# Early expert loads, padded rows left out of the gathers, shorter routing and a reordered end in a two-block transformer kernel

## What is computed

```
x = x + hybrid_mixer(rmsnorm(x))              # ends with the product y @ w_out
h = rmsnorm(x, norm_ffn_g)
grp = argmax(h @ rg_w + rg_b)                 # 1 of 4 groups
top_val, top_idx = top_k(expert logits of that group, 2)      # 2 of its 8 experts
gate = p_grp * softmax(top_val)
x = x + sum over the 2 picks: gate * (silu(h @ w_gate[e]) * (h @ w_up[e])) @ w_down[e]
out = rmsnorm(x, final_norm_g)
```

## Time and profile before

| | us |
|---|---|
| median of 3 runs | 2107.6 |
| lowest and highest of them | 2099.24, 2107.98 |
| the profiled execution, as a run | 2113.0 |
| its span in the trace | 2111.7 |

### The profile page before, as it was taken

The page is one execution under the profiler, slowest core; times in us unless marked ns, Lnnn a source line. Parts: engine busy times, 40 slices in busy tenths (PEclk is TensorE's granted clock), DMA queues, the critical chain, the costliest instruction groups (busy, mean ns, idle before and its releaser), DMA issues.

```text
span 2111.7 us, 24139 instructions
## 1 busy us (share of the span) xinstructions
PE 1889.9 (89%) x8578; PEld 1303.9 (62%) x8578; DVE 836.9 (40%) x1154; ACT 409.2 (19%) x740; POOL 969.0 (46%) x492
## 2 busy tenths in 40 slices
PE   5999999899998999999999799967589799988882
PEld 4888888787776778888888467645533333333330
DVE  5444433310444576444534797783500000100003
ACT  3111100100344422111100435523111011111011
POOL 5888887677544478888877143211110000100001
PEclk9999999999999999999999899988689899999996
DMA  3333382322111133333322122101799999999983
GB/s 125 98 99 93 103 339 99 131 90 90 60 51 50 52 94 94 96 92 99 105 96 89 44 88 60 60 30 30 301 351 391 391 396 373 388 388 399 387 359 129
DMA packets 59729, 359.60 MB, mean 170 GB/s; under 512 B 7136, under 2 KB 7520, under 8 KB 47648
## 3 DMA queue, kind: packets, MB, share of 16 engines
q1 hardware_dynamic: 45216, 317.21, 42.0%
q10 hardware_dynamic: 10192, 27.32, 3.4%
q0 software_dynamic: 4272, 14.42, 2.2%
HBM read 384.36 MB, written 27.00 MB: 195 GB/s over the span
## 4 chain that ended last, share of the span: by engine, by line
PE 70%; DMA 13%; DVE 11%; ACT 3%; issue 1%; POOL 1%; SPq 0%; DVEq 0%; ACTq 0%; POOLq 0%
PE bank L448 30%; DMA big<-w_up_in 12%; PE bank L419 11%; PE bank L1683 9%; PE bank L680 4%; PE bank L1236 3%; PE bank L1698 3%; DVE big L1013 3%; PE bank L467 2%; PE bank L1344 2%; PE bank L598 1%; DVE state L998 1%; PE bank L658 1%; ACT work L614 1%; PE bank L1624 1%
## 5 line engine op out<-in xcount | busy, mean ns | idle before, releaser
L265 POOL TENSOR_TENSOR weights_hi_parts<-ring,ones 128x1024 fp32r<-128x1024 f32 (+1 forms) x176 | 356.3, 2024 | 308.7 <-PE bank L448 138.8
L267 POOL TENSOR_TENSOR ring_parts<-ring,weights_hi_parts 128x1024 fp32r<-128x1024 f32 (+1 forms) x176 | 473.7, 2692 | 13.8
L448 PE MATMUL bank<-attention_buffers_parts,weights_hi_parts 128*128 128x512 f32 x832 | 329.5, 396 | 28.4 <-POOL ring_parts L267 17.8
L448 PE MATMUL bank<-state_parts,weights_hi_parts 128*128 128x512 f32 x832 | 326.8, 393 | 0.0
L448 PE MATMUL bank<-attention_buffers_parts,ring_parts 128*128 128x512 f32 x832 | 326.7, 393 | 0.0
L1683 PE MATMUL bank<-big,work 128*64 128x512 f32 x1040 | 295.9, 624 | 27.0 <-DMA big<-w_up_in 26.8
L419 PE MATMUL bank<-big_parts,weights_hi_parts 128*128 128x512 f32 x704 | 217.1, 390 | 1.2 <-POOL ring_parts L267 1.2
L1768 POOL TENSOR_TENSOR small<-small 128x1 f32<-128x1 f32 x36 | 6.9, 193 | 434.8 <-DVE small L1629 434.8
L448 PEld LDWEIGHTS bank<-attention_buffers_parts,weights_hi_parts 128*128 128x128 f32 x832 | 158.0, 190 | 65.1 <-POOL ring_parts L267 17.8
L852 POOL TENSOR_TENSOR ring_parts<-ring,weights_hi_parts 128x1024 fp32r<-128x1024 f32 x32 | 80.8, 2527 | 234.5 <-ACT weights_hi_parts L849 234.5
L1683 PEld LDWEIGHTS bank<-big,work 128*64 128x64 f32 x1040 | 103.3, 144 | 129.5 <-issue 121.3
(11 more groups left out here) (347 smaller groups left out, 2683.9 us busy)
## 6 DMA issues: line engine op xcount, KB each, us to landing
ring<-wdense_in SPq DMA_DIRECT2D x176, 512.0 KB, 3.6
big<-w_up_in SPq DMA_DIRECT2D x39, 2048.0 KB
state<-w_down_in SPq DMA_DIRECT2D x27, 2048.0 KB
big<-w_gate_in SPq DMA_DIRECT2D x26, 2048.0 KB
ring<-w_gate_in SPq DMA_DIRECT2D x13, 2048.0 KB
attention_buffers<-w_down_in SPq DMA_DIRECT2D x13, 2048.0 KB
ring<-wff_in SPq DMA_DIRECT2D x32, 704.0 KB, 4.1
y_rows<-big ACTq DMA_DIRECT2D x1, 12288.0 KB, 41.7
```

The source lines that it names most:

```text
L265: po.tensor_tensor(hi, raw, ones[:, 0:1].to_broadcast([128, words]), ALU.mult).then_inc(PO.sem, 1)
L267: po.tensor_tensor(lo, raw, hi.bitcast(F32), ALU.subtract) \
L448: m = pe.matmul(out, x, y_, start=j + n == 0, stop=j == len(pairs) - 1 and n == len(ts) - 1)
```

## The change

Eight edits:

1. `iota_f` and `tok_id` are made at the start of the program, right after the constants, not after the output product; every token number has 4096 (`NO_ROW`) taken off.
2. The mixer's parts of `big` are laid out anew: everything that the output product doesn't read lies in the first 2 x 4096 words. `o_gate` of head 3 goes to `rinv`. The gain goes to `work`, loaded after the last head's sums.
3. Ahead of the fifth output tile SyncE waits for the last readers of those places and then issues four expert loads: gate and up of set 0, gate of set 1, gate of set 2. Set 0's gate now lies in `attention_buffers`, its down in `ring`. After the output product come up of set 1, down of set 0, up of set 2 and then the final gain; down of sets 1 and 2 come where they came before.
4. ScalarE gets empty activations of one column (`dummy`) with Sqrt ahead of the fifth output tile, with Silu after the routing's last Exp, and with Sqrt ahead of the end.
5. The stores to `h_rows` are issued by GpSimd instead of SyncE.
6. Counting is one product of 128 columns with a reduction on VectorE behind it (4 products of 32 columns before); ranking is the triangle's product of 128 columns and 3 products of ones of 96, 64 and 32 columns (10 products of 32 columns before).
7. Empty slots get a token number above 511, and the gathers have a bounds check that leaves out such rows. The first three blocks gather all rows, and row 0 of a block is always gathered: two more VectorE operations in the routing.
8. In the end, mean and root of the tile before are issued ahead of the square of the current tile.

```diff
+    iota_f, tok_id = sb("iota_f", 128), sm(2 * NT)
+    PO.run(po.iota(iota_f[:, :].bitcast(I32), [[1, 128]], base=0, channel_multiplier=0))
+    PO.run(po.tensor_copy(iota_f[:, :], iota_f[:, :].bitcast(I32)))
+    PO.run(po.iota(tok_id[:, 0:1].bitcast(I32), [[1, 1]], base=0, channel_multiplier=1))
+    PO.run(po.tensor_copy(tok_id[:, 0:1], tok_id[:, 0:1].bitcast(I32)))
+    PO.run(po.tensor_scalar(tok_id[:, 0:1], tok_id[:, 0:1], float(-NO_ROW), None, ALU.add))
+    for t in range(1, 2 * NT):
+        numbered = PO.run(po.tensor_scalar(tok_id[:, t:t + 1], tok_id[:, 0:1], float(t % NT * 128), None, ALU.add))
...
+    sets = ((att[:, 0:WE], big[:, 4 * WE:5 * WE], ring[:, RING * SLOT - WE:RING * SLOT]),
+            (big[:, 0:WE], big[:, 2 * WE:3 * WE], res[:, 0:WE]),
+            (big[:, WE:2 * WE], big[:, 3 * WE:4 * WE], nrm[:, 0:WE]))
...
-    v2, o_gate, ym = part(4 * T), part(4 * T), part(8 * T)
+    v2, o_first = part(4 * T), part(3 * T)
+    o_gate = [chunk(o_first, 0), chunk(o_first, 1), chunk(o_first, 2), rinv[:, :]]
+    assert at_ <= 2 * WE
+    at_ = 2 * WE
+    ym = part(8 * T)
...
         if n == 4:
             until(split_u, 3)
-            AC.wait(convolved[3])
-            ffn_gain = big[:, 0:D]
+            AC.wait(summed_up[3])
+            ffn_gain = work[:, 4 * T:4 * T + D]
             ac.dma_start(ffn_gain, rows_d[:, ROWS["norm_ffn"]:ROWS["norm_ffn"] + D]).then_inc(s_gain[0], 16)
+            AC.step(ac.activation(dummy, zc, ACT.Sqrt))
+            for done in (ring_freed[23], summed_up[3], taken[3], tapped[2], tapped[3], *convolved.values()):
+                sp.wait_ge(done.queue.sem, done.value(None))
+            load_expert(0, 0, 0)
+            load_expert(1, 0, 0)
+            load_expert(0, 1, 1)
+            load_expert(0, 2, 2)
         out2_tile(24 + n, i, pair)
...
     sp.wait_ge(PE.sem, PE.n)
+    load_expert(1, 1, 1)
+    load_expert(2, 0, 0)
+    load_expert(1, 2, 2)
     sp.dma_start(final_gain, rows_d[:, ROWS["final2"]:ROWS["final2"] + D]).then_inc(s_gain[1], 16)
...
-            sp.wait_ge(DV.sem, s.value(None))
-            sp.dma_start(h_d[t * 128:(t + 1) * 128, :], h_tok[:, t * D:(t + 1) * D]).then_inc(s_hrow, 16)
+            PO.wait(s)
+            po.dma_start(h_d[t * 128:(t + 1) * 128, :], h_tok[:, t * D:(t + 1) * D]).then_inc(s_hrow, 16)
...
-    for m in range(3):
-        load_expert(m, 0, 0)
-    for b in (1, 2):
-        for m in range(2):
-            load_expert(m, b, b)
     sp.wait_ge(PE.sem, PE.n)
     load_expert(2, 1, 1)
     sp.wait_ge(s_hrow, NT * 16)
...
+    AC.step(ac.activation(dummy, zc, ACT.Silu))
...
-    for e in range(NT):
-        m = pe.matmul(banks[1][:, 0:32], ones[:, :], both[:, e * 32:(e + 1) * 32], start=e == 0, stop=e == NT - 1)
-    counted = PE.step(m)
-    for t in range(NT):
-        for e in range(t + 1):
-            m = pe.matmul(banks[0][:, t * 32:(t + 1) * 32], tri_strict[:, :] if e == t else ones[:, :],
-                          both[:, e * 32:(e + 1) * 32], start=e == 0, stop=e == t, skip_group_check=True)
+    counted = PE.step(pe.matmul(banks[1][:, 0:NT * 32], ones[:, :], both, start=True, stop=True))
+    m = pe.matmul(banks[0][:, 0:NT * 32], tri_strict[:, :], both, start=True, stop=False, skip_group_check=True)
+    for d in range(1, NT):
+        m = pe.matmul(banks[0][:, d * 32:NT * 32], ones[:, :], both[:, 0:(NT - d) * 32], start=False, stop=d == NT - 1,
+                      skip_group_check=True)
...
-    DV.run(dv.tensor_scalar(nb.bitcast(I32), banks[1][:, 0:32], float(BS - 1), None, ALU.add))
+    DV.run(dv.tensor_reduce(nb, banks[1][:, 0:NT * 32].rearrange("p (t e) -> p e t", t=NT), axis=AX.X, op=ALU.add))
+    DV.run(dv.tensor_scalar(nb.bitcast(I32), nb, float(BS - 1), None, ALU.add))
...
-    DV.run(dv.tensor_copy(slot_tok[0:BS, :].bitcast(I32), banks[2][0:BS, 0:SLOT_COLS]))
+    tokens = slot_tok[0:BS, :].bitcast(I32)
+    DV.run(dv.tensor_scalar(tokens, banks[2][0:BS, 0:SLOT_COLS], float(NO_ROW), None, ALU.add))
+    DV.run(dv.tensor_scalar(tokens[:, 0:SETS], tokens[:, 0:SETS], T - 1, None, ALU.bitwise_and))
+    DV.run(dv.tensor_scalar(tokens[0:1, :], tokens[0:1, :], T - 1, None, ALU.bitwise_and))
...
-                              bass.IndirectOffsetOnAxis(ap=idx[b][0:BS, :].bitcast(U32), axis=0)) \
+                              bass.IndirectOffsetOnAxis(ap=idx[b][0:BS, :].bitcast(U32), axis=0),
+                              bounds_check=T - 1, oob_is_err=False) \
...
+    AE.step(ac.activation(dummy, zc, ACT.Sqrt))
     for t in range(NT + 1):
+        u, r = t - 1, st[:, t - 1:t]
...
+        if t:
+            DE.wait(squares[u])
+            mean = DE.run(dv.tensor_scalar(r, r, 1.0 / D, EPS, ALU.mult, ALU.add))
+            AE.wait(mean)
+            root = AE.step(ac.activation(r, r, ACT.Sqrt))
+        if t < NT:
             AE.wait(s)
             squares.append(AE.step(ac.activation(nrm[:, t * D:(t + 1) * D], xt, ACT.Square, accum_out=st[:, t:t + 1])))
```

## The result

| | before | after |
|---|---|---|
| median of 4 runs each, us | 2107.79 | 2076.02 |
| lowest and highest | 2099.24, 2114.31 | 2074.16, 2078.65 |
| the profiled execution's span | 2111.7 | 2077.4 |
| ratio of the times, 95% interval | | 0.9853 [0.9815, 0.989] |

A forecast was written before the change was run, and what follows sets the result against it. The expert blocks were taken as bound by DMA in their first and last stretch, by TensorE in the middle. Blocks 27.1 + 21.5 = 48.6 plus end 4.0 made 52.6 us, giving 2055 us, range 2044 to 2088.

The forecast's parts named there:

- Block 0 12.3 us sooner: Before the expert blocks: shorter steps let the first gather leave 5.2 us sooner, and it lands 7.1 us faster.
- Stream 15.8 us sooner: Expert loads from block 3 on: they start 12.3 us sooner by block 0 and 3.5 by an emptied queue.
- backlog of 3.5 us: SyncE's queue when block 0 frees its set: 1.35 MB still to move before the change, nothing after it.
- Gathers 0.94 each: Blocks 3 to 38: 59% of gathered rows are skipped, saving 0.94 us per block, with ends 0.50 and 1.13.
- Middle: Blocks 13 to 25: TensorE decides, nothing is gained there, and DMA savings only shorten the load queue.
- Last stretch 21.5: Blocks 25 to 38: 8.3 us from the shortened queue plus 13.2 from 14 gathers, of 42.4 lost there.
- queue of the middle: SyncE's loads left over when the last stretch's loads begin: 1.4 matrices, 8.3 us, which the middle's gather savings remove.
- End 4.0: Final loop: with the root ahead of the square, VectorE's waits shrink to 0.34 us each, saving 4.0 us.
- (a): Rival on the gathers: skipped rows cost DMA what real ones do, only start and end gain, 2088 us; chance 0.14.
- (b): Rival before block 0: row stores on GpSimd's queue come late and hold the first gathers; 2062 at 7 us late; chance 0.06.
- (c): Rival in the blocks: all loss goes and TensorE's floor is reached, 84.0 us gained, 2024 us; chance 0.04.
- (d): Rival in the gathers: the row test makes GpSimd slow, 2156 us at 15.5 us per gather; chance 0.04.

The follow-up runs named there:

- two experiments: The changed kernel with all rows gathered again: 2096.86 us; and the kernel before with only the skipping of empty rows added: 2088.45 us.
- the experiment: The changed kernel with the end in its old order and without the Sqrt activation ahead of it: 2080.2 us in one run.

## Why the prediction was right in most terms and missed by 21 us

**Block 0 12.3 us sooner: 4.8, and the step that failed is the one that wasn't in the sum.** Its terms held: 4.2 against 0.8 + 3.45, 1.1 against 1.4 - 0.4, 7.2 against 7.1. The forecast tacitly added them to a router of 14.3 us, and that was the router of one execution, in which the clock had come back to 2.4 GHz. In the changed kernel it stayed at 1.2 GHz, 7.5 us longer; 12.3 less 7.5 is the measured 4.8 (to the tenth by luck: the terms sum to 12.5, and the output product ended 0.2 later). The hint was in the earlier trace rows: 0.50 in 1510 to 1520, so this part of the program runs with the clock low for long stretches, and whether 14.3 us would stand was a question to ask. A rival for it was missing: half clock through the router, 2055 + 7.5 = 2062.5.

**Stream 15.8 us sooner: wrong by 8.3.** The first refill left at 1543.67 instead of 1549.05, 5.4 sooner; with the backlog of 3.5 us, which is gone as forecast, 8.9. Then the engines had been idle: the row 1542 to 1548 shows a share of 0.57. That is 2.6 us of nothing, of which about 1.2 fall ahead of the refill's issue (1.67 us at 1 - 0.27, the idle share before it), so by this estimate 1.4 are lost to the restart: 7.5 instead of 15.8. A stream that has run empty doesn't start at its full rate here; the forecast counted only the gain of emptying it.

**Gathers 0.94 each: right in size, not all of it arrives.** Block 12, the last of the first stretch to start on a landing matrix, comes 14.7 us sooner; less the 7.5, 7.2 are left for 12 gathers, 0.60 each, where the forecast had 11.3 in all. With all rows gathered, that block started 5.9 us later than in the changed kernel (1695.30 against 1689.38), 0.49 each. But edit 7 alone in the kernel before brought it 10.5 us sooner (1693.57), 0.88 each, near the forecast. The other edits alone brought 8.8, and both together 14.7 and not 19.3. So the price of a gather held, and what failed is adding it to the earlier start: in this stretch the two overlap by 4.6 us. Why stays open. Between block 12 and 13 another 1.3 are lost: gate_up of block 12, behind a longer wait and so at a lower clock, took 10.04 us, and block 13 starts 14.9 us after block 12, where it was 13.6 before (1704.07 to 1717.66). Start 6.9, restart 1.4, gathers 4.1 by difference, clock 1.3 make the 13.7 missing at block 13.

**Middle: right.** 141.9 us as before, TensorE 10.00 of 10 us busy, and the DMA share down to 0.77 with the gathers thinned and at 0.99 without.

**Last stretch 21.5: 17.0.** The term for the gathers held (about 1.0 each by the queue's rate). Block 37 starts on a landing matrix in both kernels, before (first) and after:

```profile
2043.85 7.09 PE bank L1683 x32
```

```profile
2011.77 8.79 PE bank L1699 x32
```

It comes 32.1 us sooner, 18.7 of them won since block 25. Its gate_up then ran at a lower clock (8.79 against 7.09), which costs the 1.7 between 18.7 and 17.0. Less 13.2 for the gathers, 5.5 are left for the queue of the middle, where the forecast had 8.3. That term was worked out from bytes moved to one instant, 1819.5, and one matrix more or less in that count is 5.9 us, so it is too large by less than its own grain. That the skipped rows brought the stretch's gain is shown by two experiments (15.9 and 16.6 us); how it divides between gathers and queue is argued. The stretch still loses 25.4 us against TensorE's floor (179.2 against 153.8).

**End 4.0: right in size**, 3.9 in the profiles and 3.6 by the experiment. The reason was in part another: the forecast put the whole first wait of 2.61 us down to the order, but some 1.3 of it is the Sqrt table load, which edit 4 takes off that path.

**The rivals.** (a) fell with the two experiments on the gathers. (b): the stores on GpSimd's queue do land late, as this row of their line (L1442) in the changed kernel shows; before, on SyncE's, they took 2.7 us.

```profile
DMA to landing us min/median/max: 10.9/14.4/15.3
```

The last one was in at 1508.5, 20 us ahead of the first gather: no cost. For the rule weighed there (SBUF — State Buffer of the Trainium skill, the "DVE blocks DMA" trap; its 3.1 us stands in the section behind it, for a DMA beside a VectorE copy), the four issues took 0.53 to 0.83 us beside VectorE's normalising steps. Those steps are no copies, and the landings are longer than 3.1 us beside the weights in any case, so no run here tests the rule. (c) and (d) fell: TensorE still waits 30.4 us, and a gather costs GpSimd 0.93 to 1.02 us with the bounds check. On the cap of about 358 GB/s per core (DMA: Bandwidth & Descriptors of the Trainium skill, Specifications) the trace of after disagrees as that of before did: 417 GB/s over 177 us. The same page's measurements of a core alone (Bandwidth, Measured) reach 425 GB/s, and with these the trace agrees (417, and 433 over 10 us); the kernel runs on one core alone, and that was the section to weigh.

**What hadn't been seen: what block 0's start is worth.** In before the DMA engines never rest between the router and the last loads, so an earlier block 0 gives nothing: nine us sooner brought a ratio of 0.9995. In the changed kernel the sets are full before block 0, since seven of the nine loads leave ahead of the router, and the start of gate_up(0) is what restarts the stream: 10.45 us sooner brought 9.4. Either part of these loads is enough to let the engines rest: with the four issued after the product their share is 0.43 in 1530 to 1549, and with the three behind the router it is 0.11 in 1538 to 1550. Spare products that keep the router at full clock are thus worth nothing in one kernel (eleven of them) and 9.4 us in the other (six). That is also the best version measured, 2065.6 to 2066.6 us with the gap behind the output product filled.

## What to carry to other kernels

- A duration in front of the place that you change is part of your sum even if you don't touch it. Where the granted clock beside it is 0.50, price it at both levels.
- Before an early start is counted, look at what the DMA engines do until then: full engines mean that the start is worth nothing, idle ones that it is worth its whole length. A prefetch that makes them idle moves the kernel from the one case to the other, and so changes what the next edit is worth.
- Bytes that a bound stream doesn't need are worth their time wherever the stream decides, 20.8 us here for 5.3 MB. Where TensorE decides they only shorten the queue, which the next stretch gets until the queue is empty.
- Two gains in the same stream are forecast as a sum only with care: 10.5 us and 8.8 us at block 12 were 14.7 together.

## What the runs showed of the hardware

- The router's matmuls are narrow, 36 and 128 columns (groups of the changed kernel by shape, 1488 to 1508: count, busy us, mean ns):

```profile
L457 PE MATMUL bank<-small,state 128*128 128x36 f32 x64 | 13.8, 401 | 0.0
L1447 PE MATMUL bank<-ident,state 128*128 128x128 f32 x32 | 7.6, 423 | 5.8 <-DVE state L1438 5.8
```

  20 us of them without a pause didn't bring the clock from 1.2 to 2.4 GHz here, though the same work kept it at 2.4 GHz where products of 512 columns had run shortly before it. In the first profile of before 4.6 us of it (1492.0 to 1496.6) did bring the clock back. VectorE's last wait for them is 3.24 us at the one level and 6.83 at the other.
- Whether the clock comes back differs between executions of one kernel (14.3 and 21.75 us in before), and the low clock needs no load on the DMA engines (0.01 beside 0.50). What decides it stays open.
- Rows that a bounds check skips remain as packets (59729 in both kernels, 1306 more of them under 512 B), and cost next to nothing: 2.0% against 5.5% of the engines for the same 960 packets. 5.3 MB less was 20.8 us, 3.9 us per MB, where the weights at 383 to 433 GB/s take 2.3 to 2.6. So the 4 KB rows cost the stream more than their bytes.
- Four stores of 512 KB landed in 14.4 us (median) on GpSimd's queue beside a loaded SyncE queue, and in 2.7 on SyncE's own ahead of those loads.
